# Ring of eighteen slots for the weights of a two-block hybrid network, one core

## The reference

```python
# first layer, one expert e for the rows xb that chose it
g, u = jnp.split(xb @ w_up[e], 2, axis=-1)        # 1024 x 1024, hidden 512
y = (jax.nn.silu(g) * u) @ w_down[e]              # 512 x 1024

# layers two and three, for each of 4 groups g of 8 experts
a = jnp.einsum('nd,edf->nef', t, w_gate[g])       # 1024 x 256
b = jnp.einsum('nd,edf->nef', t, w_up[g])
hid = jax.nn.silu(a) * b * combine[:, g, :, None]
y = y + jnp.einsum('nef,efd->nd', hid, w_down[g]) # 256 x 1024
```

## Time and profile before

| | |
|---|---|
| median of three runs | 1779.96 us (1773.75 to 1780.94) |
| the profiled execution: its own time | 1768.81 us |
| its span, first to last instruction | 1767.0 us |
| around the span | 1.8 us |
| busy: TensorE matmul, weight load | 1406.7 us (80%), 742.5 us (42%) |
| busy: VectorE, ScalarE, GpSimd | 452.1, 396.7, 41.7 us |
| granted TensorE clock, mean | 0.897 |
| moved by DMA | 477.40 MB, 270 GB/s over the span |
| expert loops, first L965 to the next stage, about | 391 to 897, 1072 to 1319, 1489 to 1750 us |

### The profile page before, as it was taken

The page is one execution under the profiler, slowest core; times in us unless marked ns, Lnnn a source line. Parts: engine busy times, 40 slices in busy tenths (PEclk is TensorE's granted clock), DMA queues, the critical chain, the costliest instruction groups (busy, mean ns, idle before and its releaser), DMA issues.

```text
span 1767.0 us, 31246 instructions
## 1 busy us (share of the span) xinstructions
PE 1406.7 (80%) x12322; PEld 742.5 (42%) x12323; DVE 452.1 (26%) x1372; ACT 396.7 (22%) x766; POOL 41.7 (2%) x80
## 2 busy tenths in 40 slices
PE   3999988867777787798968878877789887998874
PEld 2555454443333343354546544333337534333331
DVE  0103346442111121122234522111123513121112
ACT  1101214112211121122223311222132412222221
POOL 2000201000000000000000000000000000000000
PEclk9999969978988898899979888989899887999897
DMA  9957300119999999969783125999992220779994
GB/s 325 341 193 286 89 31 0 63 61 397 410 410 410 409 410 410 410 255 410 286 335 143 53 95 224 418 417 417 418 354 101 96 76 36 286 305 418 417 418 176
DMA packets 125615, 477.40 MB, mean 270 GB/s; under 512 B 8977, under 2 KB 19470, under 8 KB 108990
## 3 DMA queue, kind: packets, MB, share of 16 engines
q1 hardware_dynamic: 122496, 468.61, 67.3%
q0 software_dynamic: 2160, 6.51, 1.3%
q10 hardware_dynamic: 910, 1.59, 0.3%
HBM read 474.71 MB, written 1.97 MB: 270 GB/s over the span
## 4 chain that ended last, share of the span: by engine, by line
PE 53%; DMA 19%; SPq 11%; issue 6%; DVE 6%; ACT 2%; PEld 2%; ACTq 0%; PEldq 0%; POOL 0%; DVEq 0%
DMA ring<-in_w_up 11%; SPq L461 10%; PE psum L1664 5%; PE psum L673 5%; PE psum L987 5%; PE psum L999 4%; DMA ring<-in_w_expert_up 4%; PE psum L974 4%; PE psum L947 3%; PE psum L1660 3%; PE psum L1017 2%; PE psum L1010 2%; DMA ring<-in_w_expert_down 2%; PE psum L1221 2%; PE psum L1233 2%
## 5 line engine op out<-in xcount | busy, mean ns | idle before, releaser
L987 PE MATMUL psum<-ring,arena 128*32 128x256 f32 x2624 | 195.9, 447 | 39.8 <-DMA ring<-in_w_expert_up 39.6
L999 PE MATMUL psum<-ring,arena 128*32 128x256 f32 x2432 | 162.4, 426 | 30.9 <-DMA ring<-in_w_up 30.7
L1142 DVE TENSOR_TENSOR arena<-arena,psum 128x128 f32<-128x128 f32 x79 | 22.8, 288 | 576.3 <-ACT arena L1077 576.3
L987 PEld LDWEIGHTS psum<-ring,arena 128*32 128x32 f32 x2624 | 86.1, 124 | 134.0 <-DMA ring<-in_w_expert_up 71.0
L999 PEld LDWEIGHTS psum<-ring,arena 128*32 128x32 f32 x2432 | 94.7, 122 | 88.5 <-issue 58.3
L974 PE MATMUL psum<-arena 32*128 32x256 f32 (+1 forms) x992 | 127.6, 469 | 2.1 <-ACT arena L1082 2.1
L947 PE MATMUL psum<-xn,arena 128*32 128x256 f32 (+1 forms) x992 | 125.8, 473 | 0.0
L965 PE MATMUL psum<-const_sb,arena 128*128 128x128 f32 x158 | 33.6, 295 | 115.2 <-issue 115.2
L1077 ACT ACTIVATE arena<-psum 128x128 f32<-128x128 f32 x79 | 21.9, 278 | 397.7 <-PE psum L987 221.7
L1077 ACT ACT_TABLE_LOAD x79 | 101.4, 1283 | 39.2 <-issue 38.9
L1664 PE MATMUL psum<-ring,hT 128*128 128x512 f32 x224 | 97.7, 593 | 0.0
(11 more groups left out here) (326 smaller groups left out, 1528.8 us busy)
## 6 DMA issues: line engine op xcount, KB each, us to landing
ring<-in_w_expert_up SPq DMA_DIRECT2D x128, 1024.0 KB, 18.2
ring<-in_w_expert_down SPq DMA_DIRECT2D x64, 1024.0 KB, 18.2
ring<-in_w_gate SPq DMA_DIRECT2D x64, 1024.0 KB, 16.1
ring<-in_w_up SPq DMA_DIRECT2D x64, 1024.0 KB, 18.0
ring<-in_w_down SPq DMA_DIRECT2D x64, 1024.0 KB, 20.4
ring<-in_w_mod SPq DMA_DIRECT2D x12, 2048.0 KB, 14.6
ring<-in_w_in SPq DMA_DIRECT2D x6, 2048.0 KB, 10.2
ring<-in_w_out SPq DMA_DIRECT2D x6, 2048.0 KB, 13.2
```

Of the source, the lines that this page charges most:

```text
L987: mm = pe.matmul(out_(j), chosen_rows(k, 0), wt[:, kk, :, j, :], start=(k == 0), stop=(k == KD - 1))
L999: mm = pe.matmul(out_(j), chosen_rows(k, e), wt, start=(k == 0), stop=(k == KD - 1))
```

## The change

The ring gets 18 slots. Slots 0 to 11 (`HOME`) are as before. Slots 12 to 17, the third round, lie in the first 12288 columns of `arena`, which now follows the ring in one allocation `store` (12 x 2048 + 23040 columns). In the dense parts that memory holds buffers of the dense layers, `hT` and `const2` among them; the buffers that live during the expert loop were moved behind it. So:

- SP loads rounds 0 and 1 as before, and the third round (round 2) after it has waited for `mixed`. Behind that it waits per piece for the use of the piece three rounds earlier instead of two.
- Dense pieces use the 12 home slots alone. Their place after an expert loop is the group of home slots that came free first.
- TensorE's loop body holds three rounds (`TURN`), so six copies of the code of a pass. 32 rounds are ten turns and two more rounds written out behind the loop; 16 rounds are five turns and one more.
- SP's loads of the first three rounds and of the last one or two are written out; its loop is over the 18 loads of three rounds.
- `const2` is overwritten by weights and loaded again for layer three: GpSimd waits for `moe_mm` (the end of TensorE's expert loop) and issues it before the loads of `pool_w`; TensorE and VectorE wait for it in both layers.
- `qk` is two buffers instead of one, `h2T` lies over `cx` instead of `hT`, and `junk`, `junk2`, `st_e`, `v2`, `probs2` and others have new places; the operations on them are the same.

```diff
-RING = 12
+HOME = 12
+RING = 18
 ROUND = 6
+TURN = RING // ROUND
...
+class Stage:
+    def __init__(self, plan, rounds, order):
+        self.rounds, self.order = rounds, order
+        self.base, self.loads, self.last = plan.n, list(plan.loads), list(plan.last)
+        self.sems = plan.sems
+    def slot(self, i, j):
+        return ROUND * self.order[i] + j
+    def landed(self, turn, i, j):
+        slot = self.slot(i, j)
+        return self.sems[f"piece{slot}"], turn * 16 + (self.loads[slot] + 16)
...
     def place(self, dmas):
-        slot = self.n % RING
+        slot = 2 * self.pos
+        self.pos = (self.pos + 1) % (HOME // 2)
+        free = max(self.last[slot:slot + 2])
         self.n += 2
+        self.last[slot:slot + 2] = [self.n, self.n]
         self.loads[slot] += 16 * dmas
-        return slot, self.sems[f"piece{slot}"], self.loads[slot]
...
+    def stage(self, rounds):
+        first = self.pos // 3
+        stage = Stage(self, rounds, (first, 1 - first, 2))
...
+        self.pos = 0 if self.last[0] < self.last[ROUND] else 3
+        return stage
...
-        ring = sb("ring", RING * SLOT).rearrange("p (r n) -> p r n", r=RING)
+        store = sb("store", HOME * SLOT + 23040)
+        ring = store[:, 0:RING * SLOT].rearrange("p (r n) -> p r n", r=RING)
+        arena = store[:, HOME * SLOT:]
...
+            for r in range(TURN):
+                if r == TURN - 1:
+
+                    sp.wait_ge(sems["mixed"], dense_done)
+                for j, src in enumerate(sources):
+                    sp.wait_ge(sems["piece_used"], max(stage.last[stage.slot(r, j)], 1))
+                    load(r, j, src[r])
+            turns = stage.rounds // TURN - 1
             with sp.Fori(0, turns) as turn:
...
-                    sp.wait_ge(sems["piece_used"], turn * len(sources) + (base + j - RING + 1))
...
+                for i in range(TURN):
+                    for j, src in enumerate(sources):
+
+                        sp.wait_ge(sems["piece_used"], turn * RING + (stage.base + ROUND * i + j + 1))
+                        load(i, j, src[bass.ds(turn * TURN + (TURN + i), 1)][0])
+            for r in range(TURN * (turns + 1), stage.rounds):
+                for j, src in enumerate(sources):
+                    sp.wait_ge(sems["piece_used"], stage.base + ROUND * (r - TURN) + j + 1)
+                    load(r % TURN, j, src[r])
...
+            turns = n_rounds // per_turn
+            with eng.Fori(0, turns) as turn:
                 for i in range(per_turn):
...
+                    one(turn, i, turn * per_turn + i)
+            for own in range(turns * per_turn, n_rounds):
+                one(turns, own % per_turn, own)
...
-            each_round(pe, at, which, 2, round_)
+            each_round(pe, at, which, TURN, round_)
...
-            pool.wait_ge(*at("fin_x"))
-            pool.dma_start(const2, ins["const2"]).then_inc(sems["const2"], 16)
             for layer in range(2):
+
+                pool.wait_ge(sems["moe_mm"], 1 + layer)
+                if layer == 0:
+                    pool.wait_ge(*at("fin_x"))
+                pool.dma_start(const2, ins["const2"]).then_inc(sems["const2"], 16)
...
-                if layer == 0:
-                    pe.wait_ge(sems["const2"], 16)
+                pe.wait_ge(sems["const2"], 16 * (1 + layer))
...
-                if layer == 0:
-                    dve.wait_ge(sems["const2"], 16)
+                dve.wait_ge(sems["const2"], 16 * (1 + layer))
```

More of the change, by code:

```diff
@@ L197, in plus @@
         return self.sems[name], self.n[name] + k
+class Stage:
[8 more added lines that the diff above has]
+        return self.sems[f"piece{slot}"], turn * 16 + (self.loads[slot] + 16)
 class Ring:
     def __init__(self, sems):
-        self.sems, self.n, self.loads = sems, 0, [0] * RING
+        self.sems, self.n, self.pos = sems, 0, 0
+        self.loads, self.last = [0] * RING, [0] * RING
     def place(self, dmas):
-        slot = self.n % RING
+        slot = 2 * self.pos
+        self.pos = (self.pos + 1) % (HOME // 2)
+        free = max(self.last[slot:slot + 2])
         self.n += 2
+        self.last[slot:slot + 2] = [self.n, self.n]
         self.loads[slot] += 16 * dmas
-        return slot, self.sems[f"piece{slot}"], self.loads[slot]
[L213 to L222, removed]
+        return slot, self.sems[f"piece{slot}"], self.loads[slot], free
+    def stage(self, rounds):
+        first = self.pos // 3
+        stage = Stage(self, rounds, (first, 1 - first, 2))
+        for r in range(rounds):
+            for j in range(ROUND):
+                slot = stage.slot(r % TURN, j)
+                self.n += 1
+                self.last[slot] = self.n
+                self.loads[slot] += 16
+        self.pos = 0 if self.last[0] < self.last[ROUND] else 3
+        return stage
 DMAS = {"mod": 1, "win": 1, "wout": 1, "win2": 1, "mla": 2, "wout2": 1}
@@ L463, in first_sources, with expert_loads, load @@
-        def first_sources():
[L465 to L471, removed]
+        def expert_loads(sp, plan, sources, dense_done):
+            stage = plan.stage(sources[0].shape[0])
+            def load(i, j, src):
+                slot = stage.slot(i, j)
+                dst = ring[:, slot, :]
+                if len(src.shape) == 3:
+                    dst = dst.rearrange("p (k n) -> p k n", k=src.shape[1])
+                sp.dma_start(dst, src).then_inc(sems[f"piece{slot}"], 16)
+            for r in range(TURN):
[5 more added lines that the diff above has]
+            turns = stage.rounds // TURN - 1
+            with sp.Fori(0, turns) as turn:
+                for i in range(TURN):
[6 more added lines that the diff above has]
+                    load(r % TURN, j, src[r])
@@ L476, in second_sources @@
                         for n in ("w_gate_2", "w_up_2"))
[L477 to L481, removed]
+            down = ins["w_down_2"][layer].rearrange("g (b e) (k p) n -> e (g b) p k n", e=2, p=P)
+            return [gate[0], up[0], gate[1], up[1], down[0], down[1]]
@@ L909, in each_round, with one @@
             eng.wait_ge(*at("ranked"))
-            with eng.Fori(0, n_rounds // per_turn) as turn:
-                for i in range(per_turn):
[L912 to L917, removed]
+            def one(turn, i, own):
+                place = slice(own, own + 1) if isinstance(own, int) else bass.ds(own, 1)
+                n = eng.value_load(extra[0:1, place], min_val=0, max_val=7)
+                with eng.If(n > 0):
+                    with eng.Fori(0, n):
+                        round_(turn, i, own, False)
+                round_(turn, i, own, True)
+            turns = n_rounds // per_turn
+            with eng.Fori(0, turns) as turn:
+                for i in range(per_turn):
+                    one(turn, i, turn * per_turn + i)
+            for own in range(turns * per_turn, n_rounds):
+                one(turns, own % per_turn, own)
         def quadrant(j):
@@ L935, in experts_pe, with slot_ready @@
             blocks = wide // P
[L936 to L941, removed]
+            stage = plan.stage(NE // at_once)
+            def slot_ready(turn, i, j):
+                pe.wait_ge(*stage.landed(turn, i, j))
+                return ring[:, stage.slot(i, j), :]
             def gather():
@@ L992, in up @@
                     for piece in range(4):
-                        slot_ready(turn, ROUND * i + piece)
-                    first = slots[ROUND * i][0]
+                        slot_ready(turn, i, piece)
+                    first = stage.slot(i, 0)
                     for k in range(KD):
@@ L1004, in down @@
                 if which == 2:
-                    pair = [slot_ready(turn, ROUND * i + 4 + e).rearrange("p (k n) -> p k n", k=2) for e in range(2)]
+                    pair = [slot_ready(turn, i, 4 + e).rearrange("p (k n) -> p k n", k=2) for e in range(2)]
                     for half in range(2):
@@ L1012, in down @@
                 for piece in range(2 if which == 1 else 0):
-                    wt = slot_ready(turn, ROUND * i + 4 + piece).rearrange("p (k n) -> p k n", k=2)
+                    wt = slot_ready(turn, i, 4 + piece).rearrange("p (k n) -> p k n", k=2)
                     for kk in range(2):
```

127 lines of the change are left out of this document (61 added, 66 removed).

## The result

| | before | after |
|---|---|---|
| median of the runs | 1776.86 us (1770.07 to 1780.94, 4 runs) | 1847.13 us (1843.27 to 1860.40, 4 runs) |
| profiled execution's span | 1767.0 us | 1843.2 us |
| mean granted TensorE clock | 0.897 | 0.879 |
| moved | 477.40 MB, 270 GB/s | 480.18 MB, 261 GB/s |
| instruction packets in queue q8 | 35 | 129 |

The ratio is 1.042 (95% interval 1.039 to 1.046): 4% slower where 2.5% faster was forecast. The dearest case of the prediction's first rival is what happened, and dearer than it was priced.

A forecast was written before the change was run, and what follows sets the result against it. The DMA was taken as the bound in the loops, TensorE from round 24 of the first layer; -15.35 - 1.65 - 2 x 15.1 + 2 = -45 gave 1735 us on the median's footing, range 1722 to 1812.

The forecast's parts named there:

- The dearest case: TensorE's first-layer loop: the dear end of rival 1, chance 0.12, left out above the range's 1812 us.
- the prediction's first rival: First-layer loop: packets refetched every turn, up to four waits of 3.1 to 4.9 us; 1750 to 1808 us; chance 0.37.
- The third round ahead of the loop: All three layers: round 2 loaded before the loop starts, saving 15.35 + 1.65 us in the first, 15.1 in each other.
- The second term: Expert loops: the deeper ring in steady state gains 0, as loads or TensorE stay the bound.
- const2, the wait for `mixed`, the new places: Outside the loops: reload hidden by 35 us of cover, waits and moved buffers cost 0; small loads 0 to +2 each.
- The code: TensorE's loop body grows from four to six copies, wanting 9 packets where 7 were held; taken as +2 us.
- 9 packets held, or one lost per turn: TensorE's first-layer loop code: the forecast case, nothing lost or 3 to 10 us; chance 0.55, by itself 1722 to 1748.
- doesn't stay: First-layer loop body not kept by TensorE, so its packets are fetched again each turn; chance 0.37.
- The rival's price: First-layer loop: 402 us of TensorE plus 36 waits of 4.5 us, 564 against 506 us; in all 1808 us.
- rival 2: Prefetch arrives only in part: some 1750 us, or 1780 if router and norm slow by the loads' length; chance 0.08.
- its two bounds: Layer three's loop: TensorE's pace would allow 17.3 us saved, the loads give 15.1.
- the 2 us: Layer three: the slack by which the DMA stays the bound over TensorE.

The follow-up runs named there:

- with 40 ahead: Kernel after with 40 adds to a semaphore nobody waits for at the start of TensorE's program: 1722.5 us, 0.969 of the kernel before.
- The runs with 40, 100 and 176 instructions: Kernel after with that many idle instructions ahead of TensorE's code: 1722.5, 1728.2 and 1788.2 us.
- with pauses and no packets: Version with 40 instructions ahead, plus loops of semaphore adds (18 and 8 iterations) ahead of each turn's first and second round: 1854.3 us, 1.045 of before.

## Why the prediction was wrong

**The third round ahead of the loop: right in sum, and in two layers of three.** -15.35 - 1.65 us were reckoned for the first layer and -15.1 for each other one. Where the code fits they were -19.9, -14.8 and -13.5, in sum -48.2 against -47.2; the span fell by 46.8 us. By layers the account was less exact. The second term, that depth in steady state is worth 0, missed perhaps 5 us in the first layer and all of layer three, where depth gave the same 13.5 us without the load ahead. The terms overlap there; the prediction took the loop as bound by its loads from its first round on.

**const2, the wait for `mixed`, the new places: right.** What lies outside the loops changed by 3 us in the kernel after and by 1.4 us with 40 ahead.

**The code: this step failed.** The term of +2 us measured 125 us, the 1847.1 us of the kernel after less the 1722.5 us of the same kernel with its code moved by 40. The counting was right: packets of 256, old body 6 + 1, new body 8 + 1, start at the end of a packet. The choice behind it was wrong. "I take +2, as the nearest rows, 476 us without a fetch, speak for a memory that keeps what it loops over": those rows were of 7 packets, and say nothing of 9. The case "9 packets held, or one lost per turn" got 0.55 and "doesn't stay" 0.37, and no row favoured the first. The runs with 40, 100 and 176 instructions and the kernel after show 7 + 1 held and 8 + 1 not. The Trainium skill, page "Runtime: NRT & Kernel Launch", section "Instruction fetch mechanics", has room for 2048 instructions in blocks of 256 as a FIFO; these runs agree with its eight blocks. They disagree with its window of two blocks: with 40 ahead, jumps over 278 instructions and back over 1672 wait for nothing once all is loaded. Nor does a plain FIFO explain that the refetch with 176 ahead stops at times.

**The rival's price: mechanism right, size off.** It said 36 waits of 4.5 us, 162 us, and TensorE's own 402 us, so 564. The sum of the waits came out near: TensorE's idle time ahead of the passes rose from 115.2 to 259.1 us, so by 144, nearly all in the first layer. This is the page's group of L1012, whose like before was L965:

```profile
L1012 PE MATMUL psum<-const_sb,store 128*128 128x128 f32 x158 | 37.3, 321 | 259.1 <-issue 259.1
```

That it came near is luck. The rival had four waits in a turn and the trace has three; it priced them at 4.5 us, and the 26 dear jumps of the first layer took 3.0 to 6.8 us, 5.9 in the mean. The two errors cancel.

The missing term is what follows a wait. The clock is at its lower level when TensorE resumes (granted 0.50 from 501.6 to 505.0 us), and the `up` part of the pass takes longer. Behind the waits of 14, 7 and 1.8 us (start us, us):

```profile
502.19 6.15 PE L1034 MATMUL psum<-store 128*32 128x256 f32 x64
...
520.77 5.40 PE L1034 MATMUL psum<-store 128*32 128x256 f32 x64
...
532.86 3.66 PE L1034 MATMUL psum<-store 128*32 128x256 f32 x64
```

That is 2.5 + 1.7 us a turn in this part; with pauses and no packets it was 1.3 + 1.4. A turn is then 30.6 + 12.3 + 5.5 + 4.2 = 52.6 of the 54.6 us measured; the prediction had 50. From its first pass to its last combine (391.8 to 1002.1 us) the loop took 610 us, 46 more than 564. Of these 38 are in the `up` matmuls, 187.9 us on the page against 41 x 3.66 = 150, and 8 are waits inside passes; what is left isn't broken down. The idle row ahead of 407.89 in the earlier trace rows and the 0.66 us beside it, against 0.41, showed that price; the sum of the rival left it out.

**The rivals' other side.** The prefetch came in whole in layers one and two, so rival 2 didn't occur. In layer three its two bounds lay as close as the 2 us said: with 40 ahead ten rounds went at TensorE's own pace (12.27 us each, 1548.04 to 1670.70 us), and then the `up` part of one waited 2.84 us for a load.

## What to carry to other kernels

Before a loop on TensorE is made longer, count its instructions in packets of 256, with the one fetched ahead: here 7 + 1 ran without a fetch, and 8 + 1 lost some 6 us at three of four jumps in a turn, with the slow clock behind it. At that edge the place of the code decides, and 40 idle instructions ahead of it were worth 125 us of 1847. And where rows show that a resource held x, they say nothing of a larger demand: such a case is priced as open, not by the nearest good row.

## What the runs showed of the hardware

- A jump into a packet that isn't there took 3.3 us with the DMA idle. With it full of weights it took mostly 5.2 to 6.8 us in the kernel after, in two cases 3.0 and 3.6 us. A jump that didn't wait took 0.2 us in the median with 40 ahead.
- Straight code waits too. In the last round of the first layer, written out behind the loop, TensorE stood 4.49 us in the middle of an `up` part in the version with 40 ahead (idle before, in brackets):

```profile
867.45 1.06 PE L1034 MATMUL psum<-store 128*32 128x256 f32 x15
...
873.01 5.75 PE L1034 MATMUL psum<-store 128*32 128x256 f32 x49 [4.49 <-issue]
```

- A pause of TensorE costs more than its length, and how much depends on what filled it. Behind 14 us of waits for packets the 64 matmuls of `up` took 6.1 us in the median of nine passes, behind 14 us of semaphore adds 5.0 us in the median of ten, and without a pause 3.66 us. Four to six us after TensorE resumed the granted clock was 0.53 behind packets (560 to 562 us) and 1.00 behind adds (564.8 to 566.8 us).
